# The causal mask of the first attention moves from two TensorE matmuls to one VectorE pass, and three queues are written in another order

## The reference

```
s = jnp.einsum('bkgqjl,...', qq, k_sel).astype(f32) * scale
s = jnp.where(tok <= t, s, MASK)          # selected keys
p = jax.nn.softmax(s, axis=-1)
...
s = jnp.einsum('bkgqd,bksd->bkgqs', qq, kw).astype(f32) * scale
p = jax.nn.softmax(jnp.where(kpos <= t, s, MASK), axis=-1)   # window keys
...
o = gg[..., 0:1] * o_cmp + gg[..., 1:2] * o_sel + gg[..., 2:3] * o_win
```

## Time and profile before

| what | before |
|---|---|
| the three runs | 2136.53, 2138.31, 2146.27 us |
| profiled execution | 2136.53 us |
| its span, first to last instruction | 2135.2 us |
| TensorE matmul busy | 2090.3 us, 98% |
| VectorE busy | 1133.3 us, 53% |
| ScalarE busy | 803.4 us, 38% |
| mean granted TensorE clock | 0.997 |
| first attention, first scores to first matmul of w_out | 202.1 to 242.8 us |

### The profile page before, as it was taken

The page is one execution under the profiler, slowest core; times in us unless marked ns, Lnnn a source line. Parts: engine busy times, 40 slices in busy tenths (PEclk is TensorE's granted clock), DMA queues, the critical chain, the costliest instruction groups (busy, mean ns, idle before and its releaser), DMA issues.

```text
span 2135.2 us, 37791 instructions
## 1 busy us (share of the span) xinstructions
PE 2090.3 (98%) x16142; PEld 1790.2 (84%) x16142; DVE 1133.3 (53%) x1781; ACT 803.4 (38%) x1171; POOL 53.9 (3%) x58
## 2 busy tenths in 40 slices
PE   7999999999999999999999999999999999999998
PEld 6987899998888888866888888888888888879998
DVE  5666765765333346675553333464333346767665
ACT  5343553553222234255432222343222224355443
POOL 0000200000000000400000000000000000200000
PEclk9999999999999999999999999999999999999999
DMA  7536755453233225259322322232232225355543
GB/s 294 218 128 219 266 182 194 160 185 139 104 106 115 85 77 127 96 185 323 125 79 80 107 99 92 82 132 99 74 113 99 86 82 160 118 207 176 181 173 112
DMA packets 66852, 303.24 MB, mean 142 GB/s; under 512 B 13728, under 2 KB 17184, under 8 KB 44960
## 3 DMA queue, kind: packets, MB, share of 16 engines
q1 hardware_dynamic: 66720, 301.34, 40.9%
HBM read 300.26 MB, written 1.05 MB: 141 GB/s over the span
## 4 chain that ended last, share of the span: by engine, by line
PE 88%; DVE 7%; ACT 2%; DMA 2%; issue 1%; SPq 0%; ACTq 0%; DVEq 0%
PE ps L489 25%; PE ps L490 25%; PE ps L491 25%; PE ps L521 2%; DVE w_lo L476 2%; PE ps L2155 1%; DMA raw<-in_w_ada 1%; DVE a_lo L1442 1%; PE ps L2444 1%; PE ps L2432 1%; PE ps L2404 1%; DVE mx L2537 1%; ACT a_hi L1342 1%; PE ps L533 1%; DVE nrm L1455 1%
## 5 line engine op out<-in xcount | busy, mean ns | idle before, releaser
L489 PE MATMUL ps<-a_hi,w_hi 128*128 128x512 f32 (+2 forms) x2120 | 725.6, 342 | 4.2 <-DVE w_lo L476 3.9
L490 PE MATMUL ps<-a_lo,w_hi 128*128 128x512 f32 (+2 forms) x2120 | 721.6, 340 | 0.0
L491 PE MATMUL ps<-a_hi,w_lo 128*128 128x512 f32 (+2 forms) x2120 | 721.4, 340 | 0.0
L476 DVE TENSOR_TENSOR w_lo<-raw,w_hi 128x2048 fp32r<-128x2048 f32 (+2 forms) x231 | 472.1, 2046 | 131.6 <-ACT w_hi L470 131.1
L470 ACT ACTIVATE w_hi<-raw 128x2048 fp32r<-128x2048 f32 (+2 forms) x229 | 391.5, 1715 | 198.6 <-PE ps L491 167.1
L489 PEld LDWEIGHTS ps<-a_hi,w_hi 128*128 128x128 f32 x2120 | 402.0, 190 | 53.1 <-DVE w_lo L476 4.2
L491 PEld LDWEIGHTS ps<-a_hi,w_lo 128*128 128x128 f32 x2120 | 402.2, 190 | 45.0
L490 PEld LDWEIGHTS ps<-a_lo,w_hi 128*128 128x128 f32 x2120 | 402.2, 190 | 44.1
L489 PE MATMUL ps<-ff_hi,w_hi 128*128 128x512 f32 (+1 forms) x880 | 306.0, 348 | 0.6 <-DVE ff_lo L999 0.3
L490 PE MATMUL ps<-ff_lo,w_hi 128*128 128x512 f32 (+1 forms) x880 | 305.0, 347 | 0.0
L491 PE MATMUL ps<-ff_hi,w_lo 128*128 128x512 f32 (+1 forms) x880 | 305.0, 347 | 0.0
(11 more groups left out here) (430 smaller groups left out, 1945.5 us busy)
## 6 DMA issues: line engine op xcount, KB each, us to landing
raw<-in_w_gu SPq DMA_DIRECT2D x110, 1024.0 KB, 4.8
raw<-in_w_ada SPq DMA_DIRECT2D x72, 1024.0 KB, 5.6
raw<-in_w_dn SPq DMA_DIRECT2D x80, 704.0 KB, 4.1
raw<-in_w_in SPq DMA_DIRECT2D x26, 1024.0 KB, 6.5
raw<-in_w_out SPq DMA_DIRECT2D x12, 1024.0 KB, 5.1
direct<-in_w_cmp SPq DMA_DIRECT2D x4, 1024.0 KB, 8.2
h<-in_x SPq DMA_DIRECT2D x2, 1024.0 KB, 7.1
nb<-in_rpb SPq DMA_DIRECT2D x32, 64.0 KB, 7.3
```

Of the source, the lines that this page charges most:

```text
L476: nc.vector.tensor_tensor(w_lo[slot][:, cols], raw[b][:, cols], w_hi[slot][:, cols].bitcast(F32), ALU.subtract).then_inc(lo_ready if done ...
L489: nc.tensor.matmul(banks[m], w1, a1, start=start and k == 0, stop=False)
L490: nc.tensor.matmul(banks[m], w1, a2, start=False, stop=False)
L491: last = nc.tensor.matmul(banks[m], w2, a1, start=False, stop=stop and k == pr.kt - 1)
```

## The change

The mask is no longer added by TensorE. `dve_max` gets one more instruction for each of the 8 jobs, a scalar_tensor_tensor: it reads the scores out of PSUM, multiplies by the scale, adds the mask and writes to a buffer in SBUF (`ss`, two of them, also used by the second block's attention). The maximum and the exponentials then read `ss`. For wide jobs the mask is a 128-column block of zeros ahead of the triangle, so the constant `causal` is 256 columns wide and the constant array grows by 64 KB.

Three queues are also written otherwise in this attention: ScalarE takes exponentials and copies in turn, one head of each, where it took both copies first; VectorE does `lower` at the end of step t, behind the weighing, where it did it in step t+1, behind the next maximum; and job 0 is weighed before the maximum of job 1, job 1 before that of job 2.

```diff
-    put("causal", np.where(f <= p, 0.0, NEG))
+    put("causal", np.concatenate([np.zeros((P, P)), np.where(f <= p, 0.0, NEG)], 1))
...
-                j.mask = None
-                j.scaled = False
+                j.mask = con("causal", P if i == 0 else 0)
+                j.scaled = True
...
-                last = nc.tensor.matmul(s_banks(key, j)[:, par, off:off + n], x.q[par], kx[par], start=off == 0,
-                                        stop=x.segs == 1, skip_group_check=x.segs == 2)
-        if x.segs == 2:
-            pe.wait_ge(ahead_ready, 2)
-            for par in range(2):
-                b = s_banks(key, j)[:, par, :].rearrange("p (b c) -> p b c", b=2)[:, :, x.width - P:x.width]
-                last = nc.tensor.matmul(b, unit_r[:], bc(ahead_r[:], 2), start=False, stop=True, skip_group_check=True)
+                last = nc.tensor.matmul(s_banks(key, j)[:, par, off:off + n], x.q[par], kx[par], start=True, stop=True)
...
-            opening = key == "first" and 2 <= t < n + 2 or t - 2 in range(EARLY_JOBS)
+            opening = t - 2 in range(EARLY_JOBS)
...
+            if x.segs == 2:
+                view = lambda b: b.rearrange("p r (b c) -> p (r b) c", b=2)[:, :, 0:x.width]
+                step(V.scalar_tensor_tensor(view(dst[:]), view(src), SCALE, bc(x.mask[:, 0:x.width], 4),
+                                            ALU.mult, ALU.add))
...
+        for t in range(first, n + 5):
+            if t < n:
+                dve_max(dve, key, t, step)
+            if first < t < n + 1:
+                dve_weigh(dve, key, t - 1, step)
+            if key == "first":
+                dve_behind(dve, t, step)
...
-            if key == "first":
-                lower(t - 1)
-                if t < n + 1:
-                    dve_weigh(dve, key, t - 1, step)
-                dve_behind(dve, t, step)
...
-        nc.scalar.activation(unit_r[:], con("ident"), ACT.Copy).then_inc(ahead_ready, 1)
-        nc.scalar.activation(ahead_r[:], con("causal"), ACT.Copy, scale=1 / SCALE).then_inc(ahead_ready, 1)
...
+        dve_weigh(dve, "first", 0, step)
         dve_max(dve, "first", 1, step)
-        dve_weigh(dve, "first", 0, step)
         split_lo(dve, ress[0].base, ress[0].loaded(0), ress[0].base % RING, CH)
+        dve_weigh(dve, "first", 1, step)
```

More of the change, by code:

```diff
@@ L43, in const_layout @@
              ("m_su", CHUNK), ("m_u", CHUNK), ("m16", CHUNK), ("moff", CHUNK), ("m16t", CHUNK),
-             ("scan0", S), ("freq", 1), ("causal", P), ("cmp_add", 2 * NCMP), ("cmp_ok", 2 * NCMP),
+             ("scan0", S), ("freq", 1), ("causal", 2 * P), ("cmp_add", 2 * NCMP), ("cmp_ok", 2 * NCMP),
              ("na_mask", S), ("cos2", S), ("sin2", S), ("pool_inv", 2 * S), ("heads", 50), ("fold", 32)]
@@ L1619, in program @@
     NJ = 24
-    unit_r = place("unit_r", [P, P], F32R)
-    ahead_r = place("ahead_r", [P, P], F32R)
     mx = place("mx", [P, 2 * NJ, 2], F32)
@@ L2297, in pe_rwkv @@
                 early_ada(pe)
-    ahead_ready = sem("ahead_ready")
     at_scores = sem("at_scores")
@@ L2529, in dve_max @@
             dst = ss[j % 2]
-            V.scalar_tensor_tensor(dst[:, :, 0:S], src[:, :, 0:S], SCALE, x.mask, ALU.mult, ALU.add)
-            step(V.tensor_scalar(dst[:, :, S:T2], src[:, :, S:T2], SCALE, None, ALU.mult))
+            if x.segs == 2:
+                view = lambda b: b.rearrange("p r (b c) -> p (r b) c", b=2)[:, :, 0:x.width]
+                step(V.scalar_tensor_tensor(view(dst[:]), view(src), SCALE, bc(x.mask[:, 0:x.width], 4),
+                                            ALU.mult, ALU.add))
+            else:
+                V.scalar_tensor_tensor(dst[:, :, 0:S], src[:, :, 0:S], SCALE, x.mask, ALU.mult, ALU.add)
+                step(V.tensor_scalar(dst[:, :, S:T2], src[:, :, S:T2], SCALE, None, ALU.mult))
             src = dst[:]
@@ L2574, in dve_attend @@
             dve.wait_ge(chunk_drained, projs[key].end)
-        def lower(t):
+        for t in range(first, n + 5):
[5 more added lines that the diff above has]
+                dve_behind(dve, t, step)
             if 4 <= t < n + 4 and t % 2:
@@ L2584, in lower @@
                                 ALU.subtract).then_inc(at_olo, 1)
-        for t in range(first, n + 5):
-            if t < n:
-                dve_max(dve, key, t, step)
-            if key == "first":
-                lower(t - 1)
-                if t < n + 1:
-                    dve_weigh(dve, key, t - 1, step)
-                dve_behind(dve, t, step)
[L2594 to L2597, removed]
         dve.wait_ge(at_pv, j0 + n)
```

## The result

| | before | after |
|---|---|---|
| median of 13 executions each | 2136.79 us | 2149.64 us |
| lowest and highest | 2134.13, 2146.27 | 2143.94, 2156.01 |
| ratio, 95% interval | | 1.0054 [1.0043, 1.0065] |
| profiled execution, its span | 2136.53, 2135.2 us | 2150.29, 2149.0 us |
| mean granted TensorE clock of it | 0.997 | 0.991 |

A forecast was written before the change was run, and what follows sets the result against it. TensorE, busy 98% of the span, bounds the kernel; the added passes make VectorE the later one up to job 5, and w_out starts 8.3 us late: 2138.3 + 8.3 = 2146.6 us, range 2140 to 2152.

The forecast's parts named there:

- rival C: TensorE drops to its lower clock in its new gaps, inside 206 to 251 us: 2156 us; chance 0.05.
- Job 0 and the queue up to max(5): VectorE up to job 5's maximum: 0.3 us late at job 0, then 5.2 us of added passes.
- rival D: The wide VectorE pass costs far more than the maximum of the same shape: 2155 us; chance 0.04.
- ScalarE's step 5: Exponentials and copies all fall between job 5's maximum and VectorE's drain: 4.1 us, plus 0.05 to hand over.
- Taking no difference: Exponentials reading SBUF instead of PSUM taken as equally long; bounds -0.9 to +0.6 us over eight on the path.
- VectorE's wait ahead of the drain: After weighing job 4, VectorE stands some 2.9 us for ScalarE, with 7.53 us of queue behind that wait.
- rival B: The new orders cost nothing, the wait ahead of the drain doesn't form: +5.3 us, 2143.6; chance 0.13.
- From nm(7) to pv(5): After job 7's maximum and negation, ScalarE's exponentials of 7 and copies of 5 in turn: 1.79 + 0.97 us.
- From pv(5) to w_out: TensorE has everything in time and needs the same 6.78 us as before; w_out starts 8.3 us late, at 251.1.
- five pieces: Forecast path from first pass to w_out's first matmul: 27.0, 4.2, 7.5, 2.85 and 6.75 us, together 48.3.

The follow-up runs named there:

- pass_twice: The changed kernel with every VectorE scale-and-mask pass done twice, the same result written again: 2158.64 us against 2139.52, ratio 1.0088.
- orders_only: The kernel before, mask matmuls kept, with the change's three new queue orders: 2142.07 us against 2137.46, ratio 1.0015.
- after_old_act: The changed kernel with ScalarE taking both copies ahead of the exponentials, as before: 2147.38 us, ratio 1.0034 to the kernel before.
- after_again: The changed kernel itself, run once more on one chip beside the kernel before: 2147.79 us against 2137.29, ratio 1.0055.
- after_filled: The changed kernel with TensorE repeating harmless transposes and scores in its holes: 2147.49 us, ratio 1.0041 to the kernel before; run again, 2147.44 us, 1.0042.
- after_old_lower: The changed kernel with `lower` (drain and low part) back behind the next maximum: 2146.3 us against 2139.52, ratio 1.0034.
- no_mask: The kernel before without its mask matmuls and nothing in their place, so its output differs: 2136.53 us against 2137.46, ratio 0.9995.
- passes_filled: passes_only with TensorE repeating transposes of job 0 and scores of job 3 in one hole: 2146.35 us against the kernel before's 2137.18, ratio 1.0045.
- passes_only: The changed kernel with the three queue orders put back as before, passes kept: 2145.66 us against the kernel before's 2137.46, ratio 1.0032.

## Why the prediction came out as it did

The forecast, slower by 8.3 us with 2140 to 2152 as the range, held the time; its size was 3 us short. That the measured 2149.64 lies within the range is in part luck, since rival C, which the range left out above, came true in part. By its own steps:

1. Job 0 and the queue up to max(5): forecast 27.0 us, measured 26.85, without a wait. `pass_twice` shows that each pass counts there in full (6.3 us for 5.9 of passes). The durations taken from the nearest rows (0.71 and 1.26 with the hand-over) were right, which also ends rival D.
2. ScalarE's step 5: 4.2 forecast, 4.41 measured. The difference is the exponentials from SBUF. In before they follow each other every 0.45 us (wide) and 0.345 (narrow), in after every 0.49 to 0.50 and 0.39 to 0.40. Taking no difference was wrong by about 0.045 us each; on eight of them that is 0.36 us. The Trainium skill ("VectorE: DVE Perf Modes", section "The TRN2 errata") gives ScalarE 52 fixed cycles more for SBUF, an estimate of 0.043 us at 1.2 GHz: the trace agrees by these intervals.
3. VectorE's wait ahead of the drain: 2.9 forecast, 3.13 measured, and 7.54 us of queue behind it against 7.53. `orders_only` (3.00 us) shows that the new order alone makes it, so rival B, in which that wait doesn't form, is out.
4. From nm(7) to pv(5): 2.85 forecast; 3.64 at the higher clock, 3.89 in after. Missed here was a wait. The transposes of job 6 stand ahead of pv(5) and can't write their bank before ScalarE has copied job 5 out of it, and each such copy now stands behind two exponentials of job 7: the waits of 1.97 and 1.06 us. `after_old_act`, where the copies go first, has 1.70 in this piece.
5. From pv(5) to w_out, "the same 6.78 us": that step failed. It is 6.78 in after_again, after_filled and after_old_lower, and 9.23 in after, 8.28 to 9.66 in others, where the clock was down. The step failed in the pace of the matmuls: 1.97 us for pv(5) instead of 1.02. This is rival C, which had a chance of 0.05. It came in part: three stretches, of which the last costs 2.45 us; the others lie beside VectorE's queue, where they cost almost nothing. It didn't reach w_out, whose matmuls follow every 0.12 us behind the first, so 2156 was too much.

What was put against rival C, that TensorE had kept its pace in one window with 1.06 us of 5 idle, was too little: after's window of 210 to 215 has 2.04 us idle, and the next is at 0.60. The new gaps were even smaller than the forecast thought, 9.8 us in 45 and none over 2.02 from 206 on, where it had 14. The chance should have been above one half: of the seven unfilled traces with a new order of ScalarE or VectorE in this table, five have a last piece over 6.78. The price was 2.7 us of path in after's trace, and some 4 in the means. The Trainium skill ("TensorE: Matmul & The Clock Gate", "What's actually happening") calls the throttled clock the default that activity releases; `after_filled`, where added activity keeps 1.00 from 210 to 260 and the mean at 0.9953, agrees.

**The sum.** In the traces the stretch grows by 51.9 - 39.5 = 12.4 us: 8.8 as forecast (its five pieces add up to 48.3), 0.9 for the missed wait and the exponentials, 2.7 for the clock. The first pass also starts 2.2 us later than the first maximum did. The passes and the orders can't be the cause: the windows show a clock of 0.73 at 200 to 205, and `no_mask`, which has neither, has 0.75 there and starts at 205.75; nor can the mask matmuls' absence, since `orders_only` has them and the lower clock too. Where the clock was at 1.00 up to there, the start was 203.26 (before) and 203.06 (`passes_filled`); all other traces had it lowered at some place ahead of 206, and start between 202.71 and 208.28. Over all executions it is 11.6 us: 7.3 between executions at an equal clock of 0.995 (few, 5 against 14), and 0.0026 of clock at 1.65 to 1.8 us per 0.001, 4.3 to 4.7. The two accounts put the share that isn't the clock at 9.3 and 7.3. The first is 49.2 - 39.5 = 9.7, less the 0.4 that scores(0) end sooner: from their start to the first pass it is 0.76 us in `passes_filled`, to the first maximum 1.18 in before. The clock of stretches that VectorE hides costs nothing on the path but counts in the mean, so the second is probably too low; how much was not measured.

**Still open.** The cost of the passes without the new orders is one: 5.6 us on the path of `passes_filled`, but at an equal clock the executions of `passes_only` are only 1.5 us (0.995, one execution) to 3.6 us (0.993, four) above those of before. And what decides whether the clock falls behind a hole is open too. `after_old_lower` stood 2.10 and 1.05 us and was busy 1.84 of 5 us, more idle than after, and kept 1.00:

```profile
240.00:245.00 5.00, 1.84 (x39) 1.22 (x40) 2.74 (x9) 3.27 (x12) 0.00 (x0) 1.00 0.97 360
245.00:250.00 5.00, 5.00 (x90) 3.78 (x94) 2.48 (x10) 2.05 (x6) 0.00 (x0) 1.00 0.32 107
```

No variant beat the kernel before. A kernel with passes for jobs 6 and 7 alone, where VectorE has idle time before, was not run: `no_mask` bounds the gain of all eight at 1.4 us of path, below what a comparison can tell.

## What to carry to other kernels

Work moved from a full engine to one that is half idle on average pays only if that one is idle in the same stretch; here VectorE, at 53% of the span, was busy 4.87 of 5 us, and every pass landed whole on the path. When a change opens holes in TensorE, price them twice: the wait itself, and, with a chance, the matmuls behind it at half the clock (here 2.45 us in one execution and none in another). Read the mean granted clock beside each time before a difference of a few us is explained, and look in every queue for what a copy or drain now stands behind.

## What the runs showed of the hardware

- The clock also fell where TensorE's row is full. At 200 to 205 after has TensorE busy 5.00 us, in part with matmuls of 2 columns, and a granted clock of 0.73:

```profile
200.00:205.00 5.00, 5.00 (x108) 4.62 (x99) 2.02 (x7) 2.25 (x4) 0.00 (x0) 0.73 0.94 348
```
```profile
200.43 1.95 PE L1785 MATMUL ps<-consts_sb,ysq 128*128 128x2 f32 x16
```

- The clock of the same program, with the same holes, fell in one execution (246.7 to 253.5) and not in another, and the executions of after spread over clocks of 0.990 to 0.996, from 2154.1 to 2144.0 us in the mean.
- A scalar_tensor_tensor with an fp32 PSUM operand, an SBUF operand and an SBUF result takes as long as a maximum over the same columns, 0.69 us for 512 and 1.22 for 1024; a broadcast mask over four groups cost nothing that shows (0.688 us, against 0.684 in the earlier trace rows).
- Repeating transposes and scores in TensorE's holes added work and yet lowered the time, by 2.6 us in the mean, with a standard error of 0.8. On the passes alone it raised the clock in the trace and did not lower the time.
